# Recurrence of two linear-attention mixers: the old state decayed on ACT, the increment added in two DVE instructions, no products with the zero state

## What is computed

```python
# GLA, by chunks of 64 tokens
inter = jnp.einsum('bhtk,bhkv->bhtv', qi * jnp.exp(b), state)
...
state = (jnp.exp(b_end[:, :, 0, :, None]) * state
         + jnp.einsum('bhsk,bhsv->bhkv', ki * jnp.exp(b_end - b), vi))
s0 = jnp.zeros((B, H, dk, dk), f32)
...
# RWKV-7, by token
sa = jnp.einsum('bhvk,bhk->bhv', state, a_t)
state = (state * w_t[:, :, None, :] + sa[..., None] * b_t[:, :, None, :]
         + v_t[..., None] * k_t[:, :, None, :])
return state, jnp.einsum('bhvk,bhk->bhv', state, r_t)
```

## Time and profile before

| | us |
|---|---|
| median of 3 runs | 1672.76 |
| the runs | 1662.93, 1672.76, 1673.29 |
| the profiled execution, its own time | 1660.9 |
| its span | 1659.2 |
| mean granted clock of PE in it | 0.969 |

### The profile page before, as it was taken

One profiled execution on the slowest core, in us unless ns is written; L12 is line 12 of the kernel. 1 busy time (PEld: TensorE's weight loads), 2 busy tenths in 40 slices (PEclk: granted clock), 3 DMA queues, 4 the chain that ended last, 5 costly groups with the idle time before them and its releaser, 6 DMA issues. The chain is left out here.

```text
span 1659.2 us, 20679 instructions
## 1 busy us (share of the span) xinstructions
PE 1542.3 (93%) x7920; PEld 1268.1 (76%) x7920; DVE 729.6 (44%) x1114; ACT 783.1 (47%) x1216; POOL 971.0 (59%) x416
## 2 busy tenths in 40 slices
PE   8999899999998989897988789999889988899998
PEld 6887787888877878676687668888667777677886
DVE  3224854551248545228565751111356555831112
ACT  5445565445455744565343334434465342434442
POOL 6887358888873578564000468878752000578785
PEclk9999999999999999999998999999999898999999
DMA  7665235556553365553301247656543101356553
GB/s 229 177 181 155 83 106 165 187 169 184 177 154 89 103 201 173 152 164 104 102 2 51 78 135 212 182 167 193 149 120 110 62 1 52 102 152 189 159 195 129
DMA packets 121632, 227.96 MB, mean 137 GB/s; under 512 B 10304, under 2 KB 26176, under 8 KB 121536
## 3 DMA queue, kind: packets, MB, share of 16 engines
q1 hardware_dynamic: 120384, 222.46, 44.4%
q10 hardware_dynamic: 1152, 4.19, 0.7%
HBM read 225.58 MB, written 1.05 MB: 137 GB/s over the span
## 5 line engine op out<-in xcount | busy, mean ns | idle before, releaser
L179 POOL TENSOR_TENSOR parts<-raw,parts 128x1024 fp32r<-128x1024 f32 (+5 forms) x412 | 970.7, 2369 | 674.0 <-ACT parts L172 672.2
L210 PE MATMUL ps<-parts,xT 128*128 128x512 f32 (+4 forms) x2624 | 822.5, 391 | 19.3 <-issue 4.5
L172 ACT CAST parts<-raw 128x1024 fp32r<-128x1024 f32 (+5 forms) x412 | 415.4, 1013 | 445.4 <-PE ps L210 243.5
L210 PEld LDWEIGHTS ps<-parts,xT 128*128 128x128 f32 x2624 | 495.0, 191 | 128.1 <-issue 13.3
L210 PE MATMUL ps<-parts,x_low 128*128 128x512 f32 (+3 forms) x672 | 255.5, 389 | 0.0
L210 PE MATMUL ps<-parts,M_low 128*128 128x512 f32 (+2 forms) x640 | 245.1, 387 | 0.0
L210 PEld LDWEIGHTS ps<-parts,x_low 128*128 128x128 f32 x672 | 129.9, 193 | 24.7 <-issue 1.5
L210 PEld LDWEIGHTS ps<-parts,M_low 128*128 128x128 f32 x640 | 121.2, 189 | 20.5
L210 PE MATMUL ps<-parts,aT 128*128 128x512 f32 x352 | 109.5, 395 | 0.0
L210 PE MATMUL ps<-parts,H_low 128*128 128x512 f32 x272 | 105.9, 394 | 0.0
L210 PEld LDWEIGHTS ps<-parts,aT 128*128 128x128 f32 x352 | 66.0, 188 | 15.6
(11 more groups left out here) (334 smaller groups left out, 1892.6 us busy)
## 6 DMA issues: line engine op xcount, KB each, us to landing
raw<-in_w_in SPq DMA_DIRECT2D x160, 512.0 KB, 3.5
raw<-in_ffn_w_down SPq DMA_DIRECT2D x44, 512.0 KB, 4.4
raw<-in_ffn_w_gate SPq DMA_DIRECT2D x40, 512.0 KB, 3.7
raw<-in_ffn_w_up SPq DMA_DIRECT2D x40, 512.0 KB, 3.7
raw<-in_w_out SPq DMA_DIRECT2D x32, 512.0 KB, 3.5
raw<-in_w_branch SPq DMA_DIRECT2D x24, 512.0 KB, 3.3
raw<-in_w_mem_kv SPq DMA_DIRECT2D x16, 512.0 KB, 3.4
raw<-in_w_in SPq DMA_DIRECT2D x16, 366.0 KB, 3.2
```

Of the source, the lines that this page charges most:

```text
L172: self.nc.scalar.copy(self.part(i, 0)[:, 0:nk, 0:w], self.raw(i)[:, 0:nk, 0:w]).then_inc(self.hi_ready.sem, 1)
L179: self.nc.gpsimd.tensor_tensor(self.part(i, 1)[:, 0:nk, 0:w], self.raw(i)[:, 0:nk, 0:w], self.part(i, 0)[:, 0:nk, 0:w], ALU.subtract).then ...
L210: ins = pe.matmul(b[:, 0:w], a(k0 + 2 * n + c, t), self.part(i, lo_w)[:, c, 0:w], start=(opens and n == p == 0), stop=(final and p == len( ...
```

## The change

- PE no longer computes unknowns(0) and from_state(0), the products with the zero state, and no longer waits for the memset of it. The last products of increment(0) wait for u0 in place of ("U", 0).
- DVE copies Q to Us for i = 0 (u0) and copies D0 into SP[1], half by half. It clears SP[1] as before and the rows Y[0:64, 0, :] that ACT no longer writes, and no longer SP[0].
- For i = 1 and 2, ACT waits until D(i-1) has been taken, then writes SP[(i + 1) % 2] = SP[i % 2] x decay in four instructions of 128x128, signalled as decayed. These stand ahead of ACT's copy of ("I", i).
- DVE then adds the increment in two instructions, one for each half, each 64 partitions x 4 blocks x 64.

```diff
--- before.py
+++ after.py
@@ -1551,8 +1551,7 @@
 
                 def unknowns(i):
                     t = i // 2
-                    if i:
-                        ST.taken(pe, ("D", i - 1))
+                    ST.taken(pe, ("D", i - 1))
                     b = TP.fill(pe, ("U", i))
                     for c in range(2):
                         ins = pe.matmul(b[:, c * P:(c + 1) * P], PTf[:, c, t * P:(t + 1) * P], SP[i % 2][:, 2 + c, :], start=True, stop=True)
@@ -1564,7 +1563,10 @@
                     for c in range(4):
                         v = H[r, t, GV + c * P:GV + (c + 1) * P] if c < 2 else VT[r, t, (c - 2) * P:(c - 1) * P]
                         pe.matmul(d[:, c * P:(c + 1) * P], KPt[r, t, c * P:(c + 1) * P], v, start=(c == 0), stop=False)
-                    TP.taken(pe, ("U", i))
+                    if i:
+                        TP.taken(pe, ("U", i))
+                    else:
+                        pe.wait_ge(*E("u0").at(1))
                     for c in range(2):
                         ins = pe.matmul(d[:, (2 + c) * P:(3 + c) * P], BAt[r, t, c * P:(c + 1) * P],
                                         Us[r, t, c * P:(c + 1) * P], start=False, stop=(c == 1))
@@ -1646,11 +1648,8 @@
                     XB.full(ins)
                 block_scores()
                 XB.drained(pe, ("P", 1))
-                pe.wait_ge(*E("state").at(1))
-                unknowns(0)
                 block_turn_p()
                 increment(0)
-                from_state(0)
                 block_values(0)
                 unknowns(1)
                 increment(1)
@@ -1942,8 +1941,13 @@
                     act.dma_start(ln[:, k, :], A[n][l].partition_broadcast(P)).then_inc(E("ln_in").sem, 16)
                 act.wait_ge(*E("pt_full").at(G2 + 1))
                 lane.done(sc.copy(spare[2][:, 256:512], ptb[:, 0:S]), E("pt"))
-                for i in range(4):
+                for i in range(1, 4):
                     r = slice(64 * (i % 2), 64 * (i % 2) + 64)
+                    if i < 3:
+                        ST.taken(act, ("D", i - 1))
+                        for c in (2, 3, 0, 1):
+                            lane.done(sc.activation(SP[(i + 1) % 2][:, c, :], SP[i % 2][:, c, :], ACT.Copy,
+                                                    scale=EP[:, c, i * CH + CH - 1:i * CH + CH]), E("decayed") if c == 1 else None)
                     if i == 3:
                         b = TP.read(act, ("n", 0))
                         lane.done(sc.copy(OT[:, 4:6, :], turned(b)), E("n_high"))
@@ -2359,8 +2363,8 @@
                 dve.wait_ge(*E("gg_sig").at(1))
                 tt(FT[:, F_GG:F_GG + 2, :], FT[:, F_GG:F_GG + 2, :], TM, ALU.mult)
                 lane.settle()
-                lane.done(v.memset(SP[0][:, :, :], 0.0))
-                lane.done(v.memset(SP[1][:, :, :], 0.0), E("state"))
+                lane.done(v.memset(SP[1][:, :, :], 0.0))
+                lane.done(v.memset(Y[0:64, 0, :], 0.0))
 
                 def norm(t):
                     yv = Y[:, t, :].rearrange("p (h d) -> p h d", d=HD)
@@ -2405,21 +2409,26 @@
 
                 def step(i):
                     t, r = i // 2, slice(64 * (i % 2), 64 * (i % 2) + 64)
-                    b = TP.read(dve, ("U", i))
                     TP.taken(dve, ("Q",))
                     q_ = Qb.rearrange("p (a c t) d -> p c a t d", a=2, c=2)[r, :, :, t, :]
-                    lane.settle()
-                    TP.empty(lane, v.tensor_tensor(Us[r, t, :].rearrange("p (c a d) -> p c a d", c=2, a=2),
-                                                   b[r, 0:256].rearrange("p (c a d) -> p c a d", c=2, a=2), q_, ALU.add), ("U", i))
+                    us = Us[r, t, :].rearrange("p (c a d) -> p c a d", c=2, a=2)
+                    if i == 0:
+                        lane.done(v.tensor_copy(us, q_), E("u0"))
+                    else:
+                        b = TP.read(dve, ("U", i))
+                        lane.settle()
+                        TP.empty(lane, v.tensor_tensor(us, b[r, 0:256].rearrange("p (c a d) -> p c a d", c=2, a=2), q_, ALU.add), ("U", i))
                     if i < 3:
                         b = ST.read(dve, ("D", i)).rearrange("p (c n) -> p c n", c=4)
-                        old, new = SP[i % 2], SP[(i + 1) % 2]
-                        for c in (2, 3, 0, 1):
-                            for hf in range(2):
-                                h = slice(64 * hf, 64 * hf + 64)
-                                ins = v.scalar_tensor_tensor(out=new[h, c, h], in0=old[h, c, h], scalar=EP[h, c, i * CH + CH - 1:i * CH + CH],
-                                                             in1=b[h, c, h], op0=ALU.mult, op1=ALU.add)
-                                lane.done(ins) if (c, hf) != (1, 1) else ST.empty(lane, ins, ("D", i))
+                        new = SP[(i + 1) % 2]
+                        if i:
+                            dve.wait_ge(*E("decayed").at(i))
+                        lane.settle()
+                        for hf in range(2):
+                            h = slice(64 * hf, 64 * hf + 64)
+                            ins = (v.tensor_tensor(new[h, :, h], new[h, :, h], b[h, :, h], ALU.add) if i else
+                                   v.tensor_copy(new[h, :, h], b[h, :, h]))
+                            ST.empty(lane, ins, ("D", i)) if hf else lane.done(ins)
 
                 step(0)
                 block_sums()
```

## The result

| | before | after |
|---|---|---|
| median, us (6 runs each) | 1668.61 | 1655.08 |
| lowest and highest run | 1662.93, 1673.29 | 1649.19, 1656.22 |
| profiled execution: its own time, span | 1660.9, 1659.2 | 1656.1, 1654.3 |
| mean granted clock in it | 0.969 | 0.966 |
| exponential to outputs(0), first layer | 22.05 | 17.04 |

The account below looks back on a forecast made before the run. Bound: a chain of latencies across PE and DVE in the stage. Gains of 4.12 + 1.6 + 1.47 = 7.2 us a layer, 14.4 for two, off the median 1672.76 give 1658.4 us; range 1645 to 1668.

Parts of the forecast that it names:

- The sum: Gains at unknowns(1), unknowns(2) and outputs(0): 4.12 + 1.6 + 1.47 = 7.2 us a layer, 14.4 us for two.
- Step 1: Start of DVE's update with the first increment: 2.51 us earlier, without the zero-state products and the memset wait.
- Step 2: Start of unknowns(1): from_state(0) goes, gain now 4.12 us; the shorter first state update is worth nothing here.
- Step 3: From unknowns(1) to the start of DVE's second update: kept at 2.84 us, its last third at the high clock.
- rival B: Low clock until second update (4.0 us), dearer decay: 6 us a layer; 1661 to 1667 with low spells downstream; chance 0.18.
- Step 4: From the start of DVE's second update to unknowns(2): 2.7 us instead of 4.31, gain 1.6 us.
- Step 5: From the start of DVE's third update to outputs(0): 1.05 us, PE late next instead of DVE; gain 1.47 us.
- Step 6: Decay on ACT: four instructions take 1.6 to 1.8 us, hidden by 2 us the first time, 1.4 the second.
- Rival A: Low clock absent or short at the stage's start: 1.8 us more a layer; 1654, or 1648 with later spells; chance 0.25.
- C: Slower: shifted later work puts low spells into the dense L210 products; chance 0.07, a third of it over 1% slower.
- The weight pipeline: Casts of the next weights and POOL behind them, after block_output(1): the whole pipeline moves forward by the same 7.2 us.

Follow-up runs that it names:

- skip_only: The change with the old eight-instruction state update in every step, no decay on ACT and one memset more; ratio to the kernel before 0.9988.
- skip_warm: skip_only with unread products in two PE waits, for the exponential and ahead of outputs(1); exponential to outputs(0) 20.74 and 21.76 us, ratio 0.9999.
- warm_two: The changed kernel with two unread products in each of two PE waits, for the exponential and ahead of outputs(1); stage 12.37 and 12.38 us, ratio 0.9853.
- before_warm2: The kernel before with three unread products in PE's 3.8 us wait and two ahead of outputs(1); stage 21.50 us in both layers, ratio 0.9974.
- before_full_warm: before_warm2 with unread products also ahead of unknowns(1), block_values(1) and the first outputs(0); stage 18.83 and 18.84 us, ratio 0.9929.
- skip_full_warm: skip_warm with unread products also ahead of unknowns(1), block_values(1) and the first outputs(0); stage 17.71 us in both layers, ratio 0.9913.

## Why the prediction was right, and where it was not

The forecast was 1658 us, the measurement 1655.08. The sum gave a ratio of 0.9914, and 0.9906 was measured. Part of this agreement is luck. The forecast stood on a median of three, 1672.76, which six runs lowered to 1668.61; and in the traces the stage gave 12.4 us where 14.4 were forecast, of which one layer gave 5.0 and the other 7.4. The chain was the right one: the second layer follows it step by step.

- **Step 1, D0.** 2.51 us earlier forecast, 2.50 in the second layer and 2.96 in the first, where the transposes (0.41 us) and the first of the increment's products were still at the high clock. In the second layer two errors cancel: from the end of the exponential to PE's first weight load it took 0.23 us and not 0.07, and from there to the increment's 0.61 and not 0.77. The copy of Q took 0.22 us, not 0.42: it reads and writes SBUF. By the Trainium skill, "VectorE: DVE Perf Modes", the section on the perf-mode tiers, a float32 copy from SBUF gets two elements a cycle and a source in PSUM only one; the trace agrees (0.22 for the copy of 64x256 in SBUF at 1392.20, 0.87 for two copies of that shape out of PSUM at 1394.55). I had priced it by the sum that reads PSUM, 0.42.
- **Step 2, unknowns(1).** 4.12 forecast, 4.21 and 4.66 measured. But its sentence "here the shorter update is worth nothing" is wrong, and by the prediction's own numbers: eight instructions from D0 = 903.94 end at 906.4, and unknowns(1) was to start at 905.79. With the eight kept (skip_only) PE waits 0.55 us for them even at the low clock, and 1.5 us in skip_warm. from_state(0) had been the cover of the slow update; taking it away uncovers it.
- **Step 3, to D1.** I kept 2.84 us. 2.70 in the second layer, 3.95 in the first, which is rival B's 4.0. This is the mis-sized term: the clock of the interval. The low spell lasted 13.7 us in the first layer, so that the whole interval was in it, and 6.8 in the second, where it held half of the interval; before it was 10.2 us.
- **Step 4, to unknowns(2).** 2.7 forecast, 2.71 in the second layer. In the first 3.62: block_values(1) starts as forecast (D1 + 1.76), but at the low clock it takes 0.9 us more, and unknowns(2) to D2 0.8 more (3.00 for 2.18). The forecast had both at the high clock.
- **Step 5, outputs(0).** D2 + 1.05 forecast, D2 + 0.92 and 0.93.
- **Step 6, the decay.** 1.28 us for four, below my lower end of 1.5. The single durations (390 ns) were the right row, but back to back the instructions overlap: four times 0.39 would be 1.56, and 0.39 with three steps of 0.30 is 1.28. Its cover held in every kernel with the decay on ACT but the one with the work tripled.
- **The sum.** 7.2 a layer forecast, 5.0 and 7.4 in the profiled execution. In the first layer D0 came 0.5 us better than forecast and the three steps behind it 1.1, 0.9 and 0.8 us worse, all at the low clock. The sum also takes 4.12 us for the zero products as if they were worth that with the slow update as well. That is the flaw that did not show in the total: skip_only gives 0.9988, not 0.995, and at the high clock the stage shows 1.1 us a layer, an estimated 1.6 without the third memset.
- **Rival A** (no low clock at the start) did not come: both layers fell to the low level. With the wait filled the stage is 12.4 us, 2.1 to 4.7 less. I had priced that state at 9.0 us a layer less than before, so 13.0, with D0 at 3.2 and D1 at 7.1 us behind the exponential, where warm_two has 2.9 and 6.6. block_sums takes 1.4 us in the traces before and after, not the 1.8 that put D1 there.
- **Rival B** came in half in the first layer: unknowns(1) to D1 at the low clock (3.95 for its 4.0), but the decay was not dearer. Its 6 us a layer were too many, 5.0 came, because the low clock went on into block_values(1) and the third increment.
- **The chances.** C gives a third of 0.07 to slower by over 1%, which is 0.02, and the summary has 0.04. Nothing hangs on it.
- **The weight pipeline** moved with the stage, as said.

That the clock falls with PE's waits, and stays up when they are filled, is shown by the pairs that differ only in filled waits (before_warm2 and before_full_warm, 0.77 and 1.00; skip_warm and skip_full_warm, 0.70 and 0.62 against 1.00). Why one wait brings a fall and a like one does not, layer by layer, is not settled.

## What to carry to other kernels

Taking work off one engine of a chain can uncover the work of another engine that had run beside it, so that the first one waits, and for PE the wait can cost the clock. So ask of each part of a change what ran beside it, and time the part alone as well; one part alone may give nothing that can be measured, as here. Where a latency chain alternates between PE and another engine, look at the granted clock of the stage beside its gaps, and price each stretch at both levels. A preparation that needs only the old value can go to an engine that is idle in the meantime; here the same work on the engine of the chain cost 4.3 us a layer, though it was shorter there. And a variant that leaves a part out must not bring in work of its own: one memset more hid 0.5 us of what was to be measured.

## What the runs showed of the hardware

- Useless work can be a gain: with nine 128x512 products a layer that nobody reads the kernel before went to 0.9929 (0.9901 to 0.9956), and with four the stage of the changed one took 12.4 us in place of 17.0 and 14.5.
- Leaving out products lengthened the low-clock time: 30.7 us in one piece (skip_only, first layer) against 10.2 before, and a mean clock of 0.957 over eleven runs against 0.963.
- Four scaled copies of 128x128 from SBUF take ACT 1.28 us back to back (0.39 each by itself) and DVE 0.87.
- Between 19 runs of the kernel before, in one series, the mean granted clock ranged from 0.951 to 0.969 and the time by 25 us, 1.5% of it, more than the effect measured here.
